# First attention layer: the queries' products run beside the key norm and the index heads' products, with banks dealt anew and another order on VectorE

## The chip, the cores and the metric

One NeuronCore of a Trainium2 chip runs the whole program. The metric is the device time of one execution in microseconds (us). The engines have queues of their own and meet at semaphores: TensorE (PE in the profile; PEld is its weight load), VectorE (DVE), ScalarE (ACT), GpSimd (POOL), and SyncE (SP), which issues the weight loads. TensorE writes to PSUM, of which there are eight banks of 512 fp32 columns; VectorE and ScalarE read them.

## What is computed

Two transformer blocks one after the other, each of depth 2, on 256 tokens of width 1024 in fp32. The change is in the first layer of the first block, sparse attention over 272 positions (16 meta tokens and 256 tokens; 384 with padding, which the kernel leaves out):

```python
q, k, v, qi, ki, wi = jnp.split(h @ w_in, list(A_SPLITS), axis=-1)
q = rope(rms_norm(q.reshape(B, T, A_Q_HEADS, HEAD_DIM), q_gain), cos, sin)     # 16 heads of 64
k = rope(rms_norm(k.reshape(B, T, A_KV_HEADS, HEAD_DIM), k_gain), cos, sin)    # 4 heads of 64
qi = rope(qi.reshape(B, T, IDX_HEADS, IDX_DIM), cos, sin)                      # 8 index heads of 64
ki = rope(ki[:, :, None, :], cos, sin)[:, :, 0, :]
...
logits = jnp.einsum('qhd,sd->qhs', qi_blk, ki_s)
score = jnp.einsum('qh,qhs->qs', w_blk, jax.nn.relu(logits))
score = jnp.where(causal, score, -jnp.inf)
_, idx = lax.top_k(score, topk)                                                # topk = 64
...
s = jnp.einsum('qgrd,qkgd->qgrk', q_blk, k_sel) * scale                        # softmax over the chosen keys, times v
```

After it come the output projection, the squared-relu MLP, a second layer with another attention, and the second block (short convolution, differential attention and two expert layers with gathered experts).

## The kernel before

*Layout.* Activations lie transposed, 128 features on the partitions and 272 positions along a row: `hTh` and `hTl` are the high and low parts of the normed input, eight chunks `kc` of 128 features each. Weights are streamed in groups `g` of four chunks `c` of 128 output columns (512 KB each) into a ring of two groups, `wring`. ScalarE makes a chunk's high part (`split_hi`, into `whi[:, c]`, which holds one group only), VectorE its low part (`split_lo`, into the place of the weights). A product is three matmuls (high times high, high times low, low times high) for each of eight `kc`: 24 matmuls, the function `chunk`, whose end raises `lin_done`. ScalarE's split of chunk c of group g waits until chunk c of group g-1 is done; SyncE's load of a chunk waits for the count of chunks done two groups earlier.

*The stage.* Groups 0 (`G_KI`), 1 (`G_QI`) and 2 (`G_KV`) give the index key, the index queries and key and value; groups 3 and 4 (`G_Q` and the next) the 16 query heads, in four pairs of chunks (a pair holds the first and second halves of four heads). Between groups 2 and 3 stand, in the queues of the engines:

- the key norm: ScalarE squares the key's two chunks (banks 0 and 1), PE sums them over heads (`pair_sums(0)`, line 753, bank 4), ScalarE takes the root (`pair_root(0)`, L1276, raises `pair_rt`), VectorE inverts it, scales the two chunks and rotates them (`pair_norm`, L1847 to L1653, raises `pair_done` to 1 and so frees banks 0 and 1);
- the index logits: 16 of them, eight heads for each of two blocks of 128 queries (n = 0 to 7 over 144 keys, n = 8 to 15 over 272). PE makes one with two fp32 matmuls on 32 rows (L773, L774; the rows' quarter is h % 4), in bank 4 + n % 4; ScalarE takes the relu (L1298) into one of two buffers `reluA`, when VectorE has used the one before last; VectorE adds it, weighted, to the score (L1878, raises `logit_used`);
- the queries, on PE: for n = 0 to 3 a chunk, the head sums of the pair before (`pair_sums(n)`, L758, twelve tiny matmuls as recorded), a chunk. The banks of the pairs are `Q_BANK` = 0, 2, 6, 0 and the next of each. ScalarE squares each chunk (L1269, L1271), takes the roots (L1279, L1280) and makes the high parts of group 4. VectorE makes the low parts of group 4 two at a time (L1616), rotates a pair (`rope_query`, L1859 to L1863) straight from the banks, and after the second pair does the selection for the first block of queries: eight rounds of the eight largest (L1701, L1702) and the mask (L1707, L1708);
- then `attention(0)`: scores (L580), masking on VectorE (L1726), the exponential (L1195), transposes (L611), values (L632). It waits for all pairs (`pair_done` 5). The selection for the second block lies inside it. Then the output projection (L664, fp32 matmuls).

PE waits for `pair_rt` 1 before the first logit and for all 16 relus before the first query chunk; `chunk` ends up behind both.

Of the kernel before, what the change touches and what calls it, by code (L numbers as in the profile page):

```python
# [127 lines left out]
def build(nc, xT_in, w_stream, wf_in, c_in, ada_w, tab_in, vec_in, alibi_in, subkeys, experts, lam_in, subln_in, out):  # L128
    ctx = ExitStack()
    with ctx:  # L130
# [302 lines left out]
        Q_BANK = (0, 2, 6, 0)  # L433
# [82 lines left out]
        def _(pe):  # L516
# [229 lines left out]
            def pair_sums(n):  # L746
# [7 lines left out]
                else:  # L754
                    heads = table("block32").rearrange("p (b c) -> p b c", b=4)[:, :, 0]
                    for r, (q0, nq) in enumerate(ROWS):
                        for half in range(2):
                            last = mm(banks[4 + n % 2][0:nq, 4 * r:4 * r + 4], sq_pair[:, n % 2, half, q0:q0 + nq], heads,  # L758
                                      start=half == 0, stop=half == 1)
# [4 lines left out]
            pe.wait_ge(pair_rt, 1)  # L764
            for n in range(2 * IDX_HEADS):
# [4 lines left out]
                if n >= 4:  # L770
                    pe.wait_ge(logit_relu, n - 3)
                bank = banks[4 + n % 4][:, 0:w]
# [3 lines left out]
            pe.wait_ge(logit_relu, 2 * IDX_HEADS)  # L776
            for n in range(4):
                g, c, b = G_Q + n // 2, 2 * (n % 2), Q_BANK[n]

                if n == 0:  # L780
                    pe.wait_ge(pair_done, 1)
                elif n == 1:
                    pe.wait_ge(v_ready, 3)
                elif n == 3:
                    pe.wait_ge(pair_done, 2)
                chunk(g, c, banks[b][:, 0:T], h_all)
                if n:
                    pair_sums(n)
                chunk(g, c + 1, banks[b + 1][:, 0:T], h_all)
# [316 lines left out]
        def _(act):  # L1106
# [158 lines left out]
            def pair_squares(n, g, c, b):  # L1265
                act.wait_ge(lin_done, CPT * g + c + 1)
                if n >= 2:
                    act.wait_ge(pair_ss, n - 1)
                link(af(sq_pair[:, n % 2, 0], banks[b][:, 0:T], ACT.Square))  # L1269
                act.wait_ge(lin_done, CPT * g + c + 2)  # L1270
                af(sq_pair[:, n % 2, 1], banks[b + 1][:, 0:T], ACT.Square).then_inc(pair_sq, 1)  # L1271

            def pair_root(n):
# [5 lines left out]
                af(q_root[0:N_META, 0, h], banks[4 + n % 2][0:N_META, 0:4], ACT.Sqrt, scale=1.0 / HD, bias=vcol("eps", 0)[0:N_META])  # L1279
                af(q_root[:, 1:3, h], banks[4 + n % 2][:, 4:12].rearrange("p (r b) -> p r b", r=2), ACT.Sqrt, scale=1.0 / HD,  # L1280
# [12 lines left out]
            for n in range(2 * IDX_HEADS):  # L1293
                w = sum(ROWS[1 + n // IDX_HEADS])
                act.wait_ge(logit_done, n + 1)
                if n >= 2:
                    act.wait_ge(logit_used, n - 1)
# [1107 lines left out]
```

## Time and profile before

| | us |
|---|---|
| median of 3 runs | 2399.63 (2394.72 to 2401.28) |
| profiled execution | 2395.71 |
| its span, first to last instruction | 2393.9 |
| stretch of the change, key sums to the first masked score | 61.92 to 115.06 |
| attention of this layer, to the output projection | 115.06 to 176.58 |

```profile
span 2393.9 us, 28234 instructions
...
PE   7779999998999998887777989987998997788776
...
DVE  5655677664778879767667476656657656676744
...
PEclk9889999989999998999999999999999999999999
```

The page cuts the span in 40 slices; each digit is the busy share of a slice in tenths, PEclk the granted TensorE clock. The stage of the change lies in the second slice (60 to 120 us). Times in the rows are us from the span's start. fp32 matmuls are recorded as two instructions each, matmuls of split values as one. Ends of matmuls are modelled, so step lengths are read from start to start.

### The profile page before, as it was taken

The page shows a single profiled execution, that of the slowest core. Times are in us where ns is not written, and L with a number is a line of the kernel's source. Part 1 is how long each engine was busy: PE and PEld are TensorE (multiplying, and loading weights), DVE is VectorE, ACT ScalarE, POOL GpSimd, SP SyncE. Part 2 cuts the span into 40 slices and gives each one's busy share as a digit, 9 for nine tenths or more (in the row PEclk, how much of TensorE's full clock was granted, in tenths as well). Part 3 has the DMA queues.
Part 4 walks back from the last instruction along what each step waited for, and adds up shares of the span by engine and source line. Part 5 has one row for each costly group of instructions (what it writes and reads, how often), then busy time and mean ns, then how long its engine had stood idle before and what let it go on. Part 6 is the DMA issues. An engine that isn't in the chain of part 4 may idle for free.

```text
span 2393.9 us, 28234 instructions
## 1 busy us (share of the span) xinstructions
PE 2093.9 (87%) x9740; PEld 1338.5 (56%) x9740; DVE 1591.5 (66%) x3698; ACT 1129.8 (47%) x2744; POOL 655.5 (27%) x624
## 2 busy tenths in 40 slices
PE   7779999998999998887777989987998997788776
PEld 7759999776999996443223434432444442233222
DVE  5655677664778879767667476656657656676744
ACT  4354534534653435444445375444457544444543
POOL 0000011110001005544443343343334344444441
PEclk9889999989999998999999999999999999999999
DMA  6205587751669756999999999999999999999995
GB/s 229 89 1 171 177 303 254 247 194 40 208 207 361 249 168 246 395 420 419 420 420 413 420 385 414 420 420 420 409 421 360 419 377 421 420 420 420 420 421 219
DMA packets 132100, 768.22 MB, mean 321 GB/s; under 512 B 14464, under 2 KB 17280, under 8 KB 60032
## 3 DMA queue, kind: packets, MB, share of 16 engines
q0 software_dynamic: 87552, 587.24, 60.3%
q1 hardware_dynamic: 43696, 177.81, 20.9%
q8 instruction: 71, 1.16, 0.2%
q10 hardware_dynamic: 720, 1.51, 0.2%
q14 instruction: 61, 0.50, 0.1%
HBM read 765.45 MB, written 1.05 MB: 320 GB/s over the span
## 4 chain that ended last, share of the span: by engine, by line
PE 52%; DMA 27%; DVE 10%; ACT 7%; issue 2%; POOL 1%; SPq 0%; ACTq 0%; POOLq 0%; DVEq 0%
DMA arena<-experts,arena 26%; PE bank L889 13%; PE bank L532 9%; PE bank L534 9%; PE bank L533 9%; PE bank L923 7%; DVE arena L2163 3%; PE bank L664 1%; ACT arena L1378 1%; ACT L1373 1%; ACT arena L1377 1%; ACT arena L1195 1%; POOL arena L498 1%; PE bank L632 1%; ACT L1449 1%
## 5 line engine op out<-in xcount | busy, mean ns | idle before, releaser
L889 PE MATMUL bank<-arena 128*128 128x512 f32 x2048 | 979.8, 616 | 165.0 <-ACT arena L1378 164.8
L2163 DVE CUSTOM_DVE_ANT_0 arena<-arena 128x1024 f32<-128x1024 f32 x512 | 633.4, 1239 | 465.4 <-DMA arena<-experts,arena 464.9
L498 POOL DMA_INDIRECT arena<-experts,arena x512 | 571.2, 1116 | 836.8 <-PE bank L889 794.9
L889 PEld LDWEIGHTS bank<-arena 128*128 128x128 f32 x2048 | 371.6, 193 | 725.4 <-ACT arena L1378 376.6
L1121 ACT CAST whi<-wring 128x1024 fp32r<-128x1024 f32 x228 | 238.2, 1049 | 271.8 <-PE bank L534 264.0
L1616 DVE TENSOR_TENSOR wlo<-wring,whi 128x1024 fp32r<-128x1024 f32 x216 | 263.3, 1224 | 144.9 <-ACT whi L1121 144.7
L1373 ACT ACTIVATE arena<-arena 128x1 f32<-128x1 f32 x512 | 102.9, 201 | 503.0 <-DVE arena L2163 501.4
L484 POOL DMA_DIRECT2D arena<-ada_w x64 | 34.2, 534 | 680.5 <-DVE adaM L1663 661.8
L1378 ACT ACTIVATE arena<-tab,arena 128x128 f32<-128x128 f32 x512 | 205.5, 401 | 16.7
L532 PE MATMUL bank<-hTh,whi 128*128 128x256 f32 (+1 forms) x576 | 172.2, 299 | 17.5 <-DVE hTl L1625 9.4
L533 PE MATMUL bank<-hTl,whi 128*128 128x256 f32 (+1 forms) x576 | 166.8, 290 | 0.0
L534 PE MATMUL bank<-hTh,wlo 128*128 128x256 f32 (+1 forms) x576 | 166.6, 289 | 0.0
L1377 ACT ACTIVATE arena<-arena 128x1 f32<-128x1 f32 x512 | 150.8, 295 | 16.7
L923 PE MATMUL bank<-wring,hfT 128*128 128x512 f32 x320 | 145.8, 599 | 3.3 <-DVE hfT L2100 3.3
L532 PE MATMUL bank<-mTh,whi 128*128 128x272 f32 (+1 forms) x512 | 146.2, 286 | 0.0
L533 PE MATMUL bank<-h1l,whi 128*128 128x272 f32 (+1 forms) x512 | 145.8, 285 | 0.0
L533 PE MATMUL bank<-mTl,whi 128*128 128x272 f32 (+1 forms) x512 | 145.8, 285 | 0.0
L532 PE MATMUL bank<-h1h,whi 128*128 128x272 f32 (+1 forms) x512 | 145.6, 284 | 0.0
L534 PE MATMUL bank<-h1h,wlo 128*128 128x272 f32 (+1 forms) x512 | 145.4, 284 | 0.0
L534 PE MATMUL bank<-mTh,wlo 128*128 128x272 f32 (+1 forms) x512 | 145.4, 284 | 0.0
L532 PEld LDWEIGHTS bank<-hTh,whi 128*128 128x128 f32 x576 | 112.6, 196 | 24.4 <-issue 18.2
L533 PEld LDWEIGHTS bank<-hTl,whi 128*128 128x128 f32 x576 | 112.9, 196 | 1.0 <-issue 1.0
(306 smaller groups left out, 3067.0 us busy)
## 6 DMA issues: line engine op xcount, KB each, us to landing
wring<-w_stream SPq DMA_DIRECT2D x236, 512.0 KB, 3.9
wring<-w_stream SPq DMA_DIRECT2D x48, 1024.0 KB
arena<-ada_w POOLq DMA_DIRECT2D x64, 512.0 KB, 5.3
alibi<-ada_w POOLq DMA_DIRECT2D x32, 512.0 KB, 5.5
arena<-experts,arena POOLq DMA_INDIRECT x512
xT<-xT_in SPq DMA_DIRECT2D x1, 1088.0 KB, 5.0
alibi<-alibi_in ACTq DMA_DIRECT2D x1, 1024.0 KB, 4.9
outT<-xT SPq DMA_DIRECT2D x2, 512.0 KB, 13.8
```

Of the source, the lines that this page charges most:

```text
L498: pool.indirect_dma_start(g_ring[:, r], None, experts[n // (2 * PEER_HEADS)], bass.IndirectOffsetOnAxis(idx[:, s // SLOTS % 2, s % SLOTS:s ...
L532: mm(dst, a[0], b[0], start=start, stop=False)
L533: mm(dst, a[0], b[1], start=False, stop=False)
L534: return mm(dst, a[1], b[0], start=False, stop=stop)
L889: last = mm(banks[2 * t + b][:, :], diag[:, r], g_ring[:, r, D + b * TILE_N:D + (b + 1) * TILE_N], start=s % SLOTS == 0, stop=s % SLOTS == ...
L923: last = mm(dst, lhs[:, 4 * half + k], w[:, k * TILE_N:(k + 1) * TILE_N], start=half == 0 and k == 0, stop=half == 1 and k == 3)
L1121: nc.scalar.copy(whi[:, c], wring[:, g % 2, c]).then_inc(hi_done, 1)
L1373: link(af(gel8[:, r:r + 1], act8[:, r:r + 1], ACT.Gelu))
L1377: link(af(coef8[:, r:r + 1], gel8[:, r:r + 1], ACT.Copy, scale=gate[:, s // SLOTS % 2, at:at + 1]))
L1378: af(diag[:, r], ident, ACT.Copy, scale=coef8[:, r:r + 1]).then_inc(diag_ready, 1)
L1616: v.tensor_tensor(wlo[:, g % 2, c], wring[:, g % 2, c], whi[:, c].bitcast(F32), ALU.subtract).then_inc(lo_done, 1)
L2163: v.tensor_tensor_reduce(g_ring[:, r, 0:D], g_ring[:, r, 0:D], hrow[:, t], 1.0, 0.0, ALU.mult, ALU.add, act8[:, r:r + 1]).then_inc(dot_don ...
```

## The change

- **PE.** The first two query chunks (group 3) follow `pair_sums(0)` at once, after a wait for the three value copies (`v_ready` 3), since they now go to banks 2 and 3. Then logits 0 and 1, the third chunk (bank 6), logits 2 and 3, `pair_sums(1)`, the fourth chunk (bank 7) with logits 4, 5 and 6 ahead of its `kc` 5, 6 and 7, and logit 7. Group 4: chunk 0 (bank 0, after `pair_done` 1) with logits 8 to 11 ahead of `kc` 4 to 7, `pair_sums(2)`, chunk 1 (bank 1) with logits 12 to 15 in the same way, then (after `pair_done` 2) chunks 2 and 3 in banks 2 and 3 with `pair_sums(3)` between, and `pair_sums(4)`.
- **Banks.** `Q_BANK` becomes 2, 6, 0, 2. Logits alternate between banks 4 and 5, so logit n waits for relu n - 2 rather than n - 4. The queries' head sums all go to bank 5, columns 288 on (`SUMS_AT`), behind the logits' 272.
- **ScalarE.** Squares, high parts of group 4, roots and relus are put in the order in which PE now makes them. The link between a pair's two squares is a wait before the second.
- **VectorE.** After the key norm: low parts 0 and 1 of group 4, the eight sums of the first block, rotation 1, low parts 2 and 3, the eight sums of the second block, rotation 2, the selection of the first block, rotations 3 and 4.

The number of instructions on each engine is the same. The diff, its core:

```diff
-        Q_BANK = (0, 2, 6, 0)
+        Q_BANK = (2, 6, 0, 2)
+        SUMS_AT = 288
...
-            pe.wait_ge(pair_rt, 1)
-            for n in range(2 * IDX_HEADS):
+            def logit(n):
...
-                if n >= 4:
-                    pe.wait_ge(logit_relu, n - 3)
-                bank = banks[4 + n % 4][:, 0:w]
+                if n == 0:
+                    pe.wait_ge(pair_rt, 1)
+                elif n >= 2:
+                    pe.wait_ge(logit_relu, n - 1)
+                bank = banks[4 + n % 2][:, 0:w]
...
-            pe.wait_ge(logit_relu, 2 * IDX_HEADS)
-            for n in range(4):
...
+            def beside(at):
+                return lambda kc: logit(at[kc]) if kc in at else None
+
+            pe.wait_ge(v_ready, 3)
+            chunk(G_Q, 0, banks[2][:, 0:T], h_all)
+            chunk(G_Q, 1, banks[3][:, 0:T], h_all)
+            logit(0)
+            logit(1)
+            chunk(G_Q, 2, banks[6][:, 0:T], h_all)
+            logit(2)
+            logit(3)
+            pair_sums(1)
+            chunk(G_Q, 3, banks[7][:, 0:T], h_all, beside({5: 4, 6: 5, 7: 6}))
+            logit(7)
+            pe.wait_ge(pair_done, 1)
+            chunk(G_Q + 1, 0, banks[0][:, 0:T], h_all, beside({4: 8, 5: 9, 6: 10, 7: 11}))
+            pair_sums(2)
+            chunk(G_Q + 1, 1, banks[1][:, 0:T], h_all, beside({4: 12, 5: 13, 6: 14, 7: 15}))
+            pe.wait_ge(pair_done, 2)
+            chunk(G_Q + 1, 2, banks[2][:, 0:T], h_all)
+            pair_sums(3)
+            chunk(G_Q + 1, 3, banks[3][:, 0:T], h_all)
             pair_sums(4)
...
+            pair_square(1, G_Q, 0, 0)
+            split_hi(G_Q + 1, 0)
+            pair_square(1, G_Q, 0, 1)
+            split_hi(G_Q + 1, 1)
+            logit_relus(0, 2)
+            pair_square(2, G_Q, 2, 0)
+            split_hi(G_Q + 1, 2)
+            pair_root(1)
+            logit_relus(2, 8)
+            pair_square(2, G_Q, 2, 1)
+            split_hi(G_Q + 1, 3)
+            logit_relus(8, 10)
+            pair_square(3, G_Q + 1, 0, 0)
+            pair_root(2)
+            logit_relus(10, 16)
+            pair_square(3, G_Q + 1, 0, 1)
+            pair_square(4, G_Q + 1, 2, 0)
+            pair_root(3)
+            pair_square(4, G_Q + 1, 2, 1)
             pair_root(4)
...
+            split_lo(G_Q + 1, 0)
+            split_lo(G_Q + 1, 1)
             dve.wait_ge(wi_ready, 1)
+            logits(1)
+            rope_query(1)
+            split_lo(G_Q + 1, 2)
+            split_lo(G_Q + 1, 3)
+            logits(2)
+            rope_query(2)
             dve.wait_ge(logit_used, 2 * IDX_HEADS)
-            for n in range(1, 5):
...
+            for _ in range(TOPK // 8):
+                select_round(1)
+            keys_selected(1)
+            rope_query(3)
+            rope_query(4)
```

## Rows read from the trace of the kernel before

**Rows 1.** the page's section 1: busy us, share of the span, instructions
```profile
PE 2093.9 (87%) x9740; PEld 1338.5 (56%) x9740; DVE 1591.5 (66%) x3698; ACT 1129.8 (47%) x2744; POOL 655.5 (27%) x624
```

**Rows 2.** busy us by stretch; columns: us, PE, PEld, DVE, ACT, POOL, PEclk, DMA
```profile
62.00:66.50 4.50, 1.00 (x5) 0.49 (x3) 2.37 (x3) 4.31 (x6) 0.00 (x0) 1.00 0.68 233
66.50:72.00 5.50, 2.04 (x24) 1.48 (x24) 5.36 (x10) 0.47 (x2) 0.00 (x0) 0.65 0.02 4
72.00:80.40 8.40, 7.42 (x41) 6.22 (x41) 6.09 (x15) 4.93 (x14) 0.00 (x0) 0.50 0.00 0
80.40:85.00 4.60, 4.60 (x20) 4.60 (x21) 0.55 (x2) 0.00 (x0) 0.00 (x0) 0.50 0.00 0
85.00:92.00 7.00, 7.00 (x59) 6.82 (x57) 1.64 (x2) 2.68 (x4) 0.00 (x0) 0.99 0.46 150
```

**Rows 3.** PE in order of time: start, us, line, xcount, idle before and its releaser
```profile
61.92 1.08 PE L753 MATMUL bank<-arena,tab 128*128 128x272 f32 x4
66.51 0.55 PE L773 MATMUL bank<-arena 32*128 32x144 f32 x8 [3.51 <-ACT rt L1276]
...
72.49 1.07 PE L773 MATMUL bank<-arena 32*128 32x144 f32 x3 [3.60 <-ACT arena L1298]
...
80.39 0.59 PE L532 MATMUL bank<-hTh,whi 128*128 128x272 f32 x1 [0.49 <-ACT arena L1298]
```

**Rows 4.** PE in order of time around pair_sums(1), full clock
```profile
91.57 0.29 PE L534 MATMUL bank<-hTh,wlo 128*128 128x272 f32 x1
91.78 1.24 PE L758 MATMUL bank<-tab,arena 128*16 128x4 f32 x12
92.89 0.37 PE L532 MATMUL bank<-hTh,whi 128*128 128x272 f32 x1
93.10 0.28 PE L533 MATMUL bank<-hTl,whi 128*128 128x272 f32 x1
...
93.48 0.29 PE L533 MATMUL bank<-hTl,whi 128*128 128x272 f32 x1
```

**Rows 5.** ScalarE in order of time, value copies and last square
```profile
62.12 0.65 ACT L1289 COPY arena<-bank 128x256 f32<-128x256 f32 x2 [2.48 <-PE bank L534]
...
110.91 0.40 ACT L1271 ACTIVATE arena<-bank 128x272 f32<-128x272 f32 x1 [2.50 <-PE bank L534]
```

**Rows 6.** VectorE in order of time, key norm to first masked score
```profile
71.21 0.43 DVE L1653 TENSOR_TENSOR arena<-arena 128x272 f32<-128x272 f32 x1
...
72.16 3.20 DVE L1878 SCALAR_TENSOR_TENSOR arena<-arena 128x144 f32<-128x144 f32 x7
...
76.68 1.71 DVE L1878 SCALAR_TENSOR_TENSOR arena<-arena 128x272 f32<-128x272 f32 x3
...
90.36 2.36 DVE L1616 TENSOR_TENSOR wlo<-wring,whi 128x1024 fp32r<-128x1024 f32 x2 [9.31 <-ACT whi L1121]
...
102.55 0.31 DVE L1701 MAX8 arena<-arena 128x8 f32<-128x144 f32 x1
...
109.17 1.73 DVE L1859 SCALAR_TENSOR_TENSOR arena<-bank,vec,tab 128x272 f32<-128x272 f32 x4
...
111.76 1.73 DVE L1859 SCALAR_TENSOR_TENSOR arena<-bank,vec,tab 128x272 f32<-128x272 f32 x4
...
115.06 0.16 DVE L1726 CUSTOM_DVE_ANT_0 arena<-bank,tab 16x16 f32<-16x16 f32 x1
```

**Rows 7.** chain of waits, fp32 matmuls of the output projection
```profile
176.58 29.60 PE bank L664 x128
```

**Rows 8.** PE, 272-column scores on 32 rows each, full clock
```profile
156.06 1.20 PE L580 MATMUL bank<-arena 32*128 32x272 f32 x16
```

**Rows 9.** shorter stretches, same columns; the last of PE alone
```profile
74.90:78.30 3.40, 3.40 (x25) 3.09 (x21) 2.28 (x5) 1.59 (x4) 0.00 (x0) 0.50 0.00 0
...
115.90:119.30 3.40, 0.83 (x20) 0.61 (x20) 3.05 (x23) 3.04 (x16) 0.00 (x0) 0.50 0.01 2
...
160.30:163.70 3.40, 1.54 (x14) 1.00 0.00 0
```

More of the change, by code:

```diff
@@ L756, in pair_sums @@
                     for r, (q0, nq) in enumerate(ROWS):
+                        at = SUMS_AT + 16 * (n - 1) + 4 * r
                         for half in range(2):
-                            last = mm(banks[4 + n % 2][0:nq, 4 * r:4 * r + 4], sq_pair[:, n % 2, half, q0:q0 + nq], heads,
+                            last = mm(banks[5][0:nq, at:at + 4], sq_pair[:, n % 2, half, q0:q0 + nq], heads,
                                       start=half == 0, stop=half == 1)
@@ L1263, in _, with pair_square @@
             act.wait_ge(v_zero, 1)
-            def pair_squares(n, g, c, b):
-                act.wait_ge(lin_done, CPT * g + c + 1)
-                if n >= 2:
+            def pair_square(n, g, c, half):
+                b = Q_BANK[n - 1] if n else 0
+                act.wait_ge(lin_done, CPT * g + c + half + 1)
+                if half == 0 and n >= 2:
                     act.wait_ge(pair_ss, n - 1)
-                link(af(sq_pair[:, n % 2, 0], banks[b][:, 0:T], ACT.Square))
-                act.wait_ge(lin_done, CPT * g + c + 2)
-                af(sq_pair[:, n % 2, 1], banks[b + 1][:, 0:T], ACT.Square).then_inc(pair_sq, 1)
+                if half:
+                    act.wait_ge(act_seq, seq[0])
+                    af(sq_pair[:, n % 2, 1], banks[b + 1][:, 0:T], ACT.Square).then_inc(pair_sq, 1)
+                else:
+                    seq[0] += 1
+                    af(sq_pair[:, n % 2, 0], banks[b][:, 0:T], ACT.Square).then_inc(act_seq, 1)
             def pair_root(n):
@@ L1292, in _, with logit_relus @@
             pair_root(0)
[L1293 to L1297, printed above, removed]
-                af(reluA[:, n % 2, 0:w], banks[4 + n % 4][:, 0:w], ACT.Relu).then_inc(logit_relu, 1)
-            for n in range(1, 5):
-                g, c = G_Q + (n - 1) // 2, 2 * ((n - 1) % 2)
-                if n >= 2:
-                    pair_root(n - 1)
-                pair_squares(n, g, c, Q_BANK[n - 1])
-                if g + 1 < G_AOUT:
-                    split_hi(g + 1, c)
-                    split_hi(g + 1, c + 1)
+            def logit_relus(n0, n1):
+                for n in range(n0, n1):
+                    w = sum(ROWS[1 + n // IDX_HEADS])
+                    act.wait_ge(logit_done, n + 1)
+                    if n >= 2:
+                        act.wait_ge(logit_used, n - 1)
+                    af(reluA[:, n % 2, 0:w], banks[4 + n % 2][:, 0:w], ACT.Relu).then_inc(logit_relu, 1)
+            pair_square(1, G_Q, 0, 0)
[17 more added lines that the diff above has]
+            pair_square(4, G_Q + 1, 2, 1)
             pair_root(4)
```

47 lines of the change are left out of this document (15 added, 32 removed).

## The prediction

> **What bounds the kernel now.** First the page: TensorE is busy 87% of the span, VectorE 66% [rows 1]. Such a share is a mean over stages and says little about one. The change touches one stage only, so I read that stage by stretches. The keys', values' and index work before it fills PE; then, from 62.0 to 80.4, PE does 1.00 us of work in 4.50, 2.04 in 5.50 and 7.42 in 8.40, and its granted clock goes from 1.00 (2.4 GHz) to 0.50 (1.2 GHz); 0.50 holds to 85.1; from there to 110.8 PE is full at 1.00 [rows 2]. PE's order of time names the two holes: 3.51 us on the root of the key norm (ScalarE) and 3.60 us on a relu that VectorE had not made room for, since VectorE was in the key norm until 71.6 [rows 3, 6]. The queries' eight chunks start only at 80.39. VectorE in turn idles 9.31 us at 81.1 to 90.4 for want of chunks, and from the selection at 102.55 on runs almost without a hole to the first masked score at 115.06 [rows 6]. So the stage ends like this: PE late, last square at 110.91, last query rotation on VectorE 111.76 to 114.35, scale of the queries to 115.06, attention.
>
> **Part by part.** All times are of the profiled execution (2395.71 us, span 2393.9; the median of the runs is 2399.63, 3.9 us more, by which I shift at the end).
>
> *Start of the queries.* The first chunk now needs the value copies, which end at 62.77, and PE is done with `pair_sums(0)` at 61.92 + 4 x 0.23 = 62.84 [rows 3, 5]. The low parts of group 3's chunks 0 and 1 are long made, those of 2 and 3 end at 66.1, before their turn. So the chunks start at 62.84 instead of 80.39, 17.5 us earlier, and the clock has no hole to fall in: the 21 matmuls that took 0.23 us each at 80.4 to 85.1 take 0.126 [rows 2, 4], 2.1 us less.
>
> *Logits inside the chunks.* What moves into PE's queue ahead of the later chunks are 16 logits, two fp32 matmuls each, which the trace records as four instructions. Before, neighbours with different heads ran on different quarters of the rows and overlapped: 16 such instructions of 272 columns took 1.20 us at full clock in the scores [rows 8], 0.30 us for the four of one logit. Now each is alone between full-array matmuls, or behind one neighbour. The nearest row for a lone one is the 272-column fp32 matmul at full clock, 128 records in 29.60 us, 0.231 each [rows 7]: 4 x 0.23 = 0.91 us per logit of the second block, and in proportion 0.49 us for 144 columns. Entering and leaving a group of small matmuls adds something: around `pair_sums(1)` the steps are 0.21 us where 0.126 is the rule, on either side, 0.17 us together [rows 4]. No row shows it for a logit. Bounds: 0.15 and 0.30 us (full overlap; I see no cause for less), and 0.66 and 1.08 us with the whole 0.17 (beyond that, a drain of the array each time: 0.75 and 1.20). I take +0.10, so 0.59 and 1.01 us.
>
> The Trainium skill, "TensorE: Matmul & The Clock Gate", Part 3 (Packing small matmuls), says that matmuls of 32 rows run together when they sit in different row groups, and that a single one takes as long as one of 128 rows. That speaks against this change, which takes them apart. The scores' 1.20 us agree with its first half, and no row here shows a lone one at full clock; by its second half the price is the 0.91 used above.
>
> *PE up to the last logit.* Five whole chunks 5 x 3.02 = 15.1 us, `pair_sums` 1 and 2 at 1.26 (start to start beyond the chunks' own step) = 2.5, seven eighths of the sixth chunk 2.65, logits 8 x 0.59 + 8 x 1.01 = 12.8: 33.1 us, so logit 15 leaves PE at about 95.9. I went through the waits on the way in that order: ScalarE's relu of logit n-2, which frees the bank of logit n, is always past (the nearest are logits 6 and 12, by some 0.7 us); `pair_done` 1 comes at 71.6, chunk 0 of group 4 starts at about 81; VectorE's low part of group 4's chunk 0 is made at 72.8; the first query rotation (`pair_done` 2) ends at about 84.6 and is wanted at 96.3.
>
> *ScalarE* gets no instruction more; it waits in another order. Behind its wait for chunk 4 stand root 2 and the relus from 10 on, and VectorE waits some 2 us there; that lies inside the time in which PE is late anyway. The table load before the key root is as before.
>
> *VectorE* works off, after the key norm: 4 low parts, 16 logit sums, rotations 1 and 2, selection, rotations 3 and 4. By the rows (7 sums of 144 columns in 3.20, 3 of 272 in 1.71, two low parts 2.3 start to start, a rotation 109.17 to 111.76) that is, without a wait, 2.3 + 8 x 0.46 + 2.59 + 2.3 + 8 x 0.60 + 2.59 + 6.62 + 2 x 2.59 = 30.0 us from 71.6: 101.6, and 0.7 for the scale of the queries. This is the floor, 102.3 against 115.06. But logit 15 comes late. Its relu is ready at 96.6 (0.27 from matmul to ScalarE, 0.4 for it), the sum ends at 97.2, and behind it VectorE has a tail with nothing left to hide it: rotation 2 (2.59), eight selection rounds and the mask (102.55 to 109.17: 6.62), rotations 3 and 4 (5.17), scale (0.7) [rows 6]. 97.2 + 15.1 = **112.3**. Before, the selection lay under PE's chunks at no cost; this is the cover that goes. PE's last chunk is done at about 103.9, its last sums at 105.6, and then it waits 6 us for VectorE.
>
> The same walk, with the half-clock steps, applied to the kernel before gives 114.9 for its 115.06, so I compare walk with walk: 114.9 - 112.3 = **2.5 us gained**. The 17.5 + 2.1 us of PE come back as 12.8 us of logits, and of the rest all but 2.5 is lost to VectorE's tail.
>
> *Weight loads and SyncE.* The loads wait for chunk counts, whose order is unchanged. They come earlier, and the next that PE could miss (group 7) waits for the output projection, after attention. Nothing. GpSimd has no work here. *Banks.* The query sums share bank 5 with odd logits; a price for writing a bank while it is read is in no row; I take 0, with up to 1 us on top.
>
> *Attention after it.* It has the same instructions (61.5 us to 176.58). Its clock is 0.50 from 115.9 to 139.8 [rows 2, 9]. With PE idle beforehand the fall comes a bit earlier, on tiny matmuls, and the return may move by a few us either way: -1 to +2 us. Value 0.
>
> Sum: 2395.7 - 2.5 = 2393.2 for an execution like the profiled one; on the median, **2397.1**.
>
> **Rivals.**
> *(a) The logits stay cheap* (0.15 and 0.30 us): something in PE still overlaps them with their neighbours. The walk then gives 103.2, 11.6 us gained, 2388.0. For it speaks only the scores' row; against it, that each stands between matmuls that use all rows.
> *(b) Switching is dearer or attention's clock returns later.* At 0.75 and 1.20 us the walk gives 115.1, no gain: PE's two holes come back spread over 16 logits. 2398 to 2401. For it: the 0.17 us steps.
> *(c) Slower: the clock falls in the mixed stretch.* Chunks 4 and 5 are about 70% logits by time. In 74.9 to 78.3 PE was busy all of 3.40 us with logits and the clock stayed at 0.50; it rose only after a dense chunk [rows 2, 9]. If it falls to 0.50 when chunk 4 starts and stays, 16 chunk steps cost 0.30 us more each and 8 logits 0.91: 4.9 + 7.3 = 12.2 us on the path that ends at logit 15, 124.5 against 114.9, 9.7 slower, 2409.3. The sign turns after 5 us at half clock (half of it is lost). Against it: with only 1.54 us of matmuls in 3.40 at 160.3 to 163.7 the clock stayed at 1.00 [rows 9], and the mixed stretch holds about 1 us of dense matmuls in that time plus the logits.
> The same page, Part 1, says that idle gaps of PE bring the lower clock back; by it the wait before attention would too, which the trace already shows for the gap at 110.8 [rows 2, 9] and which changes no price here.
> *(d) It doesn't do what it says:* PE still held up by the key norm. The diff has no wait on `pair_rt` ahead of the first two chunks, so I leave this out.
>
> **Numbers.** Forecast 0.60 (2393 to 2400 by itself, run spread included: 2394.72 to 2401.28); (b) 0.20; (a) 0.11; (c) 0.09, of which 0.06 past the bound. A measurement of this kernel can tell about 0.3%, 7.2 us, from no change. Faster by more than that: only (a) and a bit of the forecast's edge, 0.12. Slower: 0.06. Within: 0.82. Range for 8 in 10: from near (a) to past (b): 2389 to 2404.
>
> **What would show it.** PE without a hole from 61.9 to about 104, clock 1.00 throughout; lone second-block logits 0.9 to 1.1 us apart from chunk step to chunk step; the last logit relu at about 96.3; VectorE waiting on ScalarE's relus between 74 and 97, then with no hole to about 112.3; PE idle some 6 us before the first score, released by VectorE's rotation; attention 61.5 us long within 2. It is wrong if the last logit is much before 95 (a), if the clock reads 0.50 before 104 (c), or if VectorE's tail is not the last thing ahead of the first score.

## The result, and the profile after

The changed kernel took 2408.61 us (median of 20; 2402.76 to 2413.19) against 2397.72 of the kernel before (median of 20; 2392.89 to 2405.80): ratio 1.0040, 95% interval 1.0032 to 1.0048, so 0.4% slower, 9.6 us by the ratio. The profiled execution has a span of 2407.2 us. In it the key sums stand at 65.18, the first masked score at 122.92 and the output projection at 186.29: the stage took 57.7 us where before took 53.1, attention 63.4 where it took 61.5. I call "stage" here and below the time from the key sums (first record of the fp32 `pair_sums(0)`) to the first masked score, since what lies ahead of it moves from one execution to the next. One execution of all those recorded, one of the twelve of the kernel with earlier pairs below, took 2663.68 us at a mean granted clock of 0.741 and is left out of its figures.

The same view as [rows 2], the changed kernel by stretches (us, PE, PEld, DVE, ACT, POOL, PEclk, DMA share, GB/s):

```profile
62.00:66.50 4.50, 4.50 (x36) 4.17 (x35) 0.00 (x0) 1.49 (x4) 0.00 (x0) 1.00 0.05 9
...
85.00:92.00 7.00, 7.00 (x35) 4.97 (x34) 6.07 (x11) 1.98 (x4) 0.00 (x0) 1.00 0.19 73
92.00:100.00 8.00, 8.00 (x35) 6.57 (x34) 1.00 (x2) 1.40 (x6) 0.00 (x0) 0.57 0.18 66
100.00:107.00 7.00, 7.00 (x22) 4.20 (x22) 1.51 (x3) 1.18 (x4) 0.00 (x0) 0.68 0.00 0
107.00:113.00 6.00, 6.00 (x27) 5.95 (x27) 5.29 (x17) 0.77 (x2) 0.00 (x0) 0.51 0.27 90
113.00:120.00 7.00, 5.72 (x50) 5.26 (x48) 6.55 (x23) 1.93 (x7) 0.00 (x0) 0.98 0.39 136
```

Both holes of [rows 3] are gone: PE is full from 62 to 113. But the clock reads 0.57, 0.68 and 0.51 between 92 and 113, where the fifth to seventh chunk run, and PE has no hole there (8.00 us busy in 8.00, 7.00 in 7.00): it goes through 35 matmuls in 8 us at 92 and 22 in 7 us at 100. In the trace's record of the clock it is 0.50 from 92.3 to 99.2 and from 102.6 to 112.8. Before the first fall PE did logits 8 to 11, one ahead of each step of the chunk; before it came back at 99.2, head sums and four steps of the sixth chunk in a row (95.36 to 98.36).

PE in order of time, the start of the queries, with logits 0 and 1 side by side:

```profile
65.18 1.08 PE L754 MATMUL bank<-arena,tab 128*128 128x272 f32 x4
66.08 0.39 PE L533 MATMUL bank<-hTh,whi 128*128 128x272 f32 x1
...
72.10 0.29 PE L535 MATMUL bank<-hTh,wlo 128*128 128x272 f32 x1
72.32 0.52 PE L777 MATMUL bank<-arena 32*128 32x144 f32 x4
72.67 0.42 PE L778 MATMUL bank<-arena 32*128 32x144 f32 x4
73.02 0.39 PE L533 MATMUL bank<-hTh,whi 128*128 128x272 f32 x1
73.25 0.29 PE L534 MATMUL bank<-hTl,whi 128*128 128x272 f32 x1
```

The chunks start 0.90 us after the key sums, as forecast. Below, a matmul of a chunk takes 0.126 us from start to start at the full clock, and a step of the chunk (one `kc`) is three of them, 0.38 us. The two adjacent logits of 144 columns stretch the row of the chunk's matmuls (72.10 to 73.25, less two of 0.126) by 0.90 us, both together. Now a lone one of 272 columns, logit 8 ahead of the fifth step of chunk 4:

```profile
86.05 0.29 PE L535 MATMUL bank<-hTh,wlo 128*128 128x272 f32 x1
86.27 0.72 PE L777 MATMUL bank<-arena 32*128 32x272 f32 x2
86.84 0.62 PE L778 MATMUL bank<-arena 32*128 32x272 f32 x2
87.38 0.39 PE L533 MATMUL bank<-hTh,whi 128*128 128x272 f32 x1
87.61 0.29 PE L534 MATMUL bank<-hTl,whi 128*128 128x272 f32 x1
```

From 86.05 to 87.61 there are 1.56 us where two matmuls of 0.126 would be: 1.31 us for one logit. The chunk's last matmul ahead of it takes 0.22 to the logit's start, the logit's second pair of records comes 0.57 after the first and the chunk's next matmul 0.54 after that, where two fp32 records last 0.46, and the matmul after that follows at 0.23: 0.39 us in all on top of 4 x 0.23. Lone logits of 144 columns stand 1.26 us apart, start to start, with a chunk step of 0.38 between: 0.88 us. VectorE's tail, which answers to [rows 6]:

```profile
107.40 0.50 DVE L1914 SCALAR_TENSOR_TENSOR arena<-arena 128x272 f32<-128x272 f32 x1 [2.58 <-ACT arena L1322]
107.82 1.72 DVE L1895 SCALAR_TENSOR_TENSOR arena<-bank,vec,tab 128x272 f32<-128x272 f32 x4
...
117.03 1.72 DVE L1895 SCALAR_TENSOR_TENSOR arena<-bank,vec,tab 128x272 f32<-128x272 f32 x4
...
119.62 1.73 DVE L1895 SCALAR_TENSOR_TENSOR arena<-bank,vec,tab 128x272 f32<-128x272 f32 x4
...
122.92 0.16 DVE L1762 CUSTOM_DVE_ANT_0 arena<-bank,tab 16x16 f32<-16x16 f32 x1
```

The last sum is 107.40 to 107.90; rotation 2, selection to 116.9, rotations 3 and 4, the scale, and the first masked score: 15.5 us from start to start, 15.7 forecast. PE waits 3.0 us for it, not 6, since it is later itself (view of the waits, 60 to 124 us):

```profile
PE bank L581 <- DVE arena L1899: 3.0, 1, 3.0
```

### The profile page after: what moved, and what is told of

Same layout as the page of the kernel before. It is cut to its first block, busy times and chain, and to the rows that moved or that the text cites. A ratio compares the mean times of both kernels' runs of the same rounds, so it can differ in the third digit from the quotient of the medians.

```text
span 2407.2 us, 28235 instructions
## 1 busy us (share of the span) xinstructions
PE 2117.4 (88%) x9740; PEld 1352.1 (56%) x9740; DVE 1591.2 (66%) x3698; ACT 1128.9 (47%) x2744; POOL 640.2 (27%) x624
## 3 DMA queue, kind: packets, MB, share of 16 engines
q1 hardware_dynamic: 43696, 177.81, 20.6%
## 4 chain that ended last, share of the span: by engine, by line
PE 55%; DMA 25%; DVE 8%; ACT 8%; issue 2%; POOL 1%; SPq 0%; ACTq 0%; POOLq 0%; DVEq 0%
DMA arena<-experts,arena 25%; PE bank L905 13%; PE bank L533 9%; PE bank L535 9%; PE bank L534 9%; PE bank L939 7%; DVE arena L2205 3%; PE bank L665 1%; ACT arena L1414 1%; ACT L1409 1%; ACT arena L1413 1%; POOL arena L499 1%; ACT arena L1211 1%; PE bank L633 1%; ACT L1485 1%
## 5 line engine op out<-in xcount | busy, mean ns | idle before, releaser
L499 POOL DMA_INDIRECT arena<-experts,arena x512 | 556.3, 1086 | 853.5 <-PE bank L905 812.2
```

The costliest lines, as they stand in the source:

```text
L499: pool.indirect_dma_start(g_ring[:, r], None, experts[n // (2 * PEER_HEADS)], bass.IndirectOffsetOnAxis(idx[:, s // SLOTS % 2, s % SLOTS:s ...
```

## The experiments

*The theories.* P: a lone logit on a quarter of the rows costs more than taken (0.88 and 1.31 us), PE is late by that. C: the clock falls because of such logits, and this makes the loss. D: VectorE's order, with the selection in its tail, makes it.

The walk of the prediction (times added up along the queues of PE, ScalarE and VectorE, each wait met by what ends it) was repeated for each kernel with the prices measured in these traces and a clock of 1.00. It is an estimate, and the yardstick of the table; "low" is the time in us at a granted clock of 0.50 inside the stage, from the record of the clock. In the kernels with the new order 1.8 to 5.9 us of it lie in the wait before attention, behind PE's own work (1.2 in the block, none with the selection early).

| kernel | stage, walk | stage, measured | low in it | attention | ratio to before (95%) |
|---|---|---|---|---|---|
| before | 52.9 | 53.1 | 17.1 | 61.5 | 1 |
| before, second profile | 52.9 | 53.7 | 22.4 | 64.0 | |
| before, third profile | 52.9 | 53.2 | 17.1 | 61.5 | |
| changed | 53.4 | 57.7 | 20.3 | 63.4 | 1.0040 (1.0032 to 1.0048) |
| changed, again | 53.4 | 57.8 | 20.6 | 63.2 | 1.0044 (1.0028 to 1.0060) |
| pairs | 46.1 | 46.1 | 5.9 | 61.5 | 0.9988 (0.9977 to 0.9999) |
| pairs, again | 46.1 | 46.1 | 4.9 | 64.0 | 0.9984 (0.9969 to 0.9998) |
| pairs, earlier | 45.8 | 48.5 | 12.0 | 64.0 | 0.9981 (0.9967 to 0.9996) |
| full rows | 48.9 | 48.7 | 5.0 | 64.0 | 1.0001 (0.9991 to 1.0011) |
| full rows, padded | 55.9 | 55.8 | 4.0 | 62.3 | 1.0020 (1.0003 to 1.0038) |
| block | 44.7 | 51.2 | 14.8 | 62.1 | 1.0012 (0.9999 to 1.0025) |
| block on full rows | 47.9 | 48.0 | 4.0 | 62.3 | 0.9986 (0.9970 to 1.0002) |
| selection early | 51.3 | 62.3 | 30.7 | 61.6 | 1.0041 (1.0025 to 1.0057) |
| spread | 54.1 | 71.8 | 51.1 | 63.4 | 1.0039 (1.0016 to 1.0061) |

(Before's walk has its half-clock steps in it, so its 17.1 us don't stand against it.)

The table has one profile of each kernel or two. The mean granted clock is on record for every execution, and tells how long each ran at half clock. Averaged over the executions of a kernel that is 185 and 182 us for the changed kernel, 181 for the block, 183 with the selection early; 187 for the spread logits; 175, 176 and 174 for the kernel before beside them; 170 and 168 for the pairs, 174 for the earlier ones; 167, 166 and 172 for the three kernels with logits on all rows. Each is known to 2 to 6 us. So the difference between lone logits on a quarter of the rows and logits on all rows is in the executions without a profile too.

### Logits in pairs

```diff
-            chunk(G_Q, 3, banks[7][:, 0:T], h_all, beside({5: 4, 6: 5, 7: 6}))
-            logit(7)
+            chunk(G_Q, 3, banks[7][:, 0:T], h_all, beside({5: (4, 5), 7: (6, 7)}))
...
-            chunk(G_Q + 1, 0, banks[0][:, 0:T], h_all, beside({4: 8, 5: 9, 6: 10, 7: 11}))
+            chunk(G_Q + 1, 0, banks[0][:, 0:T], h_all, beside({4: (8, 9), 6: (10, 11)}))
...
-            chunk(G_Q + 1, 1, banks[1][:, 0:T], h_all, beside({4: 12, 5: 13, 6: 14, 7: 15}))
+            chunk(G_Q + 1, 1, banks[1][:, 0:T], h_all, beside({4: (12, 13), 6: (14, 15)}))
```

> The changed kernel, but the logits from the fourth on stand in pairs instead of alone: 4 and 5, 6 and 7 in the fourth chunk, 8 and 9, 10 and 11 in the fifth, 12 and 13, 14 and 15 in the sixth. Neighbours of a pair are on different quarters of the rows. Theory P (price of a lone logit): in the changed kernel's trace a lone logit lengthens the chunk by 1.31 us (272 columns) or 0.88 us (144), while the two adjacent ones at 72.3 us cost 0.90 us together. So a pair should cost about 0.90 or 1.33 us, as much as one alone: six visits less, the walk through the queues ends the stage 7.3 us earlier than in the changed kernel, total 7 to 10 us below the changed kernel. Theory D (VectorE's order, with the selection in its tail, is the cause): VectorE's tail is untouched, total within 2 us of the changed kernel. Theory C (the clock alone): the price per pair is of no matter, the clock still falls to 0.50 in the fifth and sixth chunk, total 0 to 4 us below the changed kernel.

PE in order of time around logits 8 and 9, and VectorE's first masked score, of this kernel:

```profile
80.50 0.29 PE L535 MATMUL bank<-hTh,wlo 128*128 128x272 f32 x1
80.72 0.73 PE L777 MATMUL bank<-arena 32*128 32x272 f32 x4
81.28 0.63 PE L778 MATMUL bank<-arena 32*128 32x272 f32 x4
81.84 0.39 PE L533 MATMUL bank<-hTh,whi 128*128 128x272 f32 x1
...
107.49 0.16 DVE L1761 CUSTOM_DVE_ANT_0 arena<-bank,tab 16x16 f32<-16x16 f32 x1
```

From 80.50 to the last matmul before the next pair, at 82.58, there are 2.08 us, less six matmuls of 0.126: 1.32 us for two logits, as much as one alone cost. The stage is 46.1 us, on the walk, the clock 1.00 until PE's end at 100.9 (it falls at 101.6). Total 2392.50 us against 2396.21, and 12.5 us below the changed kernel by the two ratios of 1.0040 and 0.9988. That is more than P foresaw (7 to 10) and much more than D did (within 2), so D falls: VectorE's order is the same here. The clock, which by C should have fallen all the same, held. So price and clock changed together, and this run alone doesn't part them: of the 11.6 us by which the stage is shorter than the changed kernel's, 7.3 are price by the walk and 4.3 the clock.

### Logits on all 128 rows

```diff
-                mm(bank, qiA[g, 2 * (h // 4), q0:w], kiA[g, 0, 0:w], start=True, stop=False)
-                mm(bank, qiA[g, 2 * (h // 4) + 1, q0:w], kiA[g, 1, 0:w], start=False, stop=True).then_inc(logit_done, 1)
+                mm(bank, qiA[:, 2 * (h // 4), q0:w], kiA[:, 0, 0:w], start=True, stop=False)
+                mm(bank, qiA[:, 2 * (h // 4) + 1, q0:w], kiA[:, 1, 0:w], start=False, stop=True).then_inc(logit_done, 1)
```

> The changed kernel, but each logit's two matmuls take all 128 rows instead of 32, so that they sum four heads: the scores are not the reference's (that part of the computation is changed), the columns, the order and all waits are the same. Theory C (the clock falls because matmuls on a quarter of the rows do not hold it): the granted clock reads 1.00 through the mixed stretch, no chunk step of 0.23 us in it, total 3 to 6 us below the changed kernel. Theory P with the switch between quarter rows and full rows as its cause: the price of a logit falls from 1.31 to about 0.91 + 0.17 = 1.08 us, another 3 us. If the price is that of fp32 between split values whatever the rows, it stays at 1.31. If the clock falls all the same, the rows are not what it looks at.

PE in order of time around one logit, then PE by stretches (us, PE, PEclk, DMA share, GB/s), of this kernel:

```profile
82.58 0.29 PE L535 MATMUL bank<-hTh,wlo 128*128 128x272 f32 x1
82.71 0.62 PE L777 MATMUL bank<-arena 128*128 128x272 f32 x2
83.17 0.62 PE L778 MATMUL bank<-arena 128*128 128x272 f32 x2
...
83.88 0.29 PE L535 MATMUL bank<-hTh,wlo 128*128 128x272 f32 x1
...
84.00:88.00 4.00, 4.00 (x30) 1.00 0.08 14
88.00:92.00 4.00, 4.00 (x27) 1.00 0.32 117
92.00:96.00 4.00, 4.00 (x27) 1.00 0.10 16
```

82.58 to 83.88 is 1.30 us, less three matmuls of 0.126 is 0.92 us: exactly four fp32 records, no switch at all, where P had put 1.08. So the 0.4 us belong to going between quarter rows and full rows, not to fp32 beside split values. The clock is 1.00 through the same mixture, and PE has no hole in either kernel up to its last 0.49 us wait, at 102.0 here and at 117.5 in the changed kernel. The stage is 48.7 us, total 2396.06 against 2396.21. This kernel comes near the one that the prediction described (it took 0.59 and 1.01 us a logit; here it is 0.49 and 0.92, at a clock of 1.00). Even so the total is level with before's (1.0001), though the stage is 4.4 us shorter.

### All logits in one block

```diff
-            logit(0)
-            logit(1)
             chunk(G_Q, 2, banks[6][:, 0:T], h_all)
-            logit(2)
-            logit(3)
             pair_sums(1)
-            chunk(G_Q, 3, banks[7][:, 0:T], h_all, beside({5: 4, 6: 5, 7: 6}))
-            logit(7)
...
+            chunk(G_Q, 3, banks[7][:, 0:T], h_all)
+            pe.wait_ge(pair_rt, 2)
+            for n in range(2 * IDX_HEADS):
+                logit(n)
             pe.wait_ge(pair_done, 1)
-            chunk(G_Q + 1, 0, banks[0][:, 0:T], h_all, beside({4: 8, 5: 9, 6: 10, 7: 11}))
+            chunk(G_Q + 1, 0, banks[0][:, 0:T], h_all)
+            pe.wait_ge(logit_relu, 2 * IDX_HEADS)
             pair_sums(2)
...
             logits(1)
+            logits(2)
             rope_query(1)
             split_lo(G_Q + 1, 2)
             split_lo(G_Q + 1, 3)
-            logits(2)
             rope_query(2)
```

(ScalarE's order follows; the logits of the sixth chunk are taken out in the same way.)

> One part of the change alone: the first four query chunks run ahead of the logits, with the new banks, but the 16 logits then stand in one block (two banks), followed by the other four chunks; VectorE sums all logits before the first rotation. No logit is inside a chunk. Theory P: the logits overlap again and cost about 9 us in all, the walk ends the stage 8.7 us before the changed kernel's and 8 us before the kernel before; total 2386 to 2395 where before is 2398. Theory D (the order on VectorE with the selection after PE's last sums): the selection is in the tail here too, so no gain over the kernel before. Theory C: the clock falls only if PE waits in the block; total some us above the first figure if it does.

The kernel by stretches, columns as above:

```profile
79.50:83.30 3.80, 2.79 (x24) 2.18 (x24) 2.21 (x6) 1.84 (x8) 0.00 (x0) 0.99 0.44 138
83.30:86.60 3.30, 2.82 (x11) 2.02 (x11) 1.17 (x3) 1.05 (x4) 0.00 (x0) 0.50 0.02 5
```

The walk's 44.7 us became 51.2. PE had only 2.79 us of work, all logits, in 79.5 to 83.3, and the clock then read 0.50 until 96.9: PE went on with logits, with holes of 0.2 to 0.3 us between every four matmuls, to 93.9. Total 2400.93 against 2396.21, ratio 1.0012. Of the gain that P foresaw 6.5 us are missing in the stage, and with all rows the same block stays on its walk (below): the clock took them.

### The selection early

```diff
             split_lo(G_Q + 1, 2)
             split_lo(G_Q + 1, 3)
+            dve.wait_ge(logit_used, IDX_HEADS)
+            for _ in range(TOPK // 8):
+                select_round(1)
+            keys_selected(1)
             logits(2)
             rope_query(2)
-            dve.wait_ge(logit_used, 2 * IDX_HEADS)
-            for _ in range(TOPK // 8):
-                select_round(1)
-            keys_selected(1)
             rope_query(3)
```

> The changed kernel, but VectorE makes the selection of the first block of queries (it needs logits 0 to 7 only) before the sums of the second block, in time in which it waits for relus. Theory P: the last logit is late whatever VectorE does; what is saved is only the part of the tail that lies behind PE's own end, 2 us by the walk: total 1 to 3 us below the changed kernel. Theory D: the whole selection of 6.6 us leaves the path, total 6 us or more below the changed kernel.

```profile
92.00:96.00 4.00, 4.00 (x15) 2.54 (x15) 3.59 (x14) 0.40 (x1) 0.00 (x0) 0.50 0.00 0
...
112.00:116.00 4.00, 4.00 (x19) 4.00 (x19) 3.73 (x9) 0.56 (x2) 0.00 (x0) 0.50 0.40 131
```

(By stretches, as above.) The ratio is that of the changed kernel, 1.0041: neither D's 6 us nor P's 1 to 3 are there. But the run says little of either, since the clock moved too: in this profiled execution the stage was 62.3 us, 11 over its walk, with the clock at 0.50 from 82.8 to 116.9 but for 3.4 us. What rules D out is the run with pairs.

### The changed kernel again

> The changed kernel itself once more, beside the others on one chip, for a second look at its clock. Theory C+P (a lone quarter-row logit costs 1.31 and 0.88 us, and the clock falls in the mixed stretch on top): the stage from the key sums to the first masked score is 53.4 us by the walk plus what the low clock adds, 57.7 in the first look; the fall lies again between the fifth and the seventh chunk, though not at the same instruction. Total 9 to 12 us above the kernel before.

2409.53 us against 2400.00 on the same chip, 1.0044. Stage 57.8 us; the clock was 0.50 from 91.2 to 98.0 and from 101.4 to 111.7, at the same two places as in the first profile (92.3 to 99.2, 102.6 to 112.8).

### The block on full rows

The edits of the block and of the full rows together.

> The kernel with all 16 logits in one block, but each logit on all 128 rows, so that no two overlap (scores not the reference's, that part of the computation is changed). Theory C: the clock reads 1.00 in the block and after it, where the quarter rows had 0.50 from 83.3 to 96.9; the stage is 47.9 us by the walk against 51.2 measured with quarter rows, though PE's own work in the block is longer; total 3 us or more below the block with quarter rows. If the clock follows PE's idle time alone, the result is the other way round: the block gets 2 to 4 us longer, since the overlap is gone.

```profile
80.00:84.00 4.00, 3.37 (x25) 2.94 (x24) 2.15 (x6) 2.23 (x7) 0.00 (x0) 1.00 0.40 131
84.00:88.00 4.00, 4.00 (x20) 3.31 (x20) 1.96 (x6) 1.77 (x5) 0.00 (x0) 1.00 0.02 4
```

(By stretches, as above.) The clock is 1.00 in and after the block. The stage is 48.0 us, 3.2 less than with quarter rows though the logits no longer overlap, and the total 2395.90 against 2400.00. The two blocks differ in nothing but the rows in the program. In the trace the holes differ too: with quarter rows 2.79 us of work in 3.80, here 3.37 in 4.00. So this pair alone leaves room for PE's idle time. The changed kernel and the one on full rows don't: PE has no hole in either before the clock falls in one of them, and in the other it doesn't fall.

### Pairs, earlier in their chunks

```diff
-            chunk(G_Q, 3, banks[7][:, 0:T], h_all, beside({5: (4, 5), 7: (6, 7)}))
+            chunk(G_Q, 3, banks[7][:, 0:T], h_all, beside({3: (4, 5), 6: (6, 7)}))
...
-            chunk(G_Q + 1, 0, banks[0][:, 0:T], h_all, beside({4: (8, 9), 6: (10, 11)}))
+            chunk(G_Q + 1, 0, banks[0][:, 0:T], h_all, beside({2: (8, 9), 5: (10, 11)}))
...
-            chunk(G_Q + 1, 1, banks[1][:, 0:T], h_all, beside({4: (12, 13), 6: (14, 15)}))
+            chunk(G_Q + 1, 1, banks[1][:, 0:T], h_all, beside({1: (12, 13), 4: (14, 15)}))
```

> The kernel with logits in pairs, each pair placed two or three steps of the chunk earlier (4 and 5 ahead of step 3, 6 and 7 ahead of 6, then 2 and 5, then 1 and 4). By the walk the stage is 45.8 us where the pairs had 46.1: no difference to be measured, total about 2392, unless the clock falls on the denser mixture, which would cost 3 us or more.

```profile
92.00:96.00 4.00, 4.00 (x17) 0.50 0.00 0
96.00:100.00 4.00, 4.00 (x18) 0.50 0.00 0
```

(PE by stretches.) The clock did fall, 90.7 to 101.0, and the stage took 48.5 us for a walk of 45.8. Total 2395.52 us against 2400.00, ratio 0.9981: no difference from the pairs that the intervals show. So pairs don't hold the clock wherever they stand.

### The lone logits spread

```diff
-            chunk(G_Q, 3, banks[7][:, 0:T], h_all, beside({5: 4, 6: 5, 7: 6}))
-            logit(7)
+            chunk(G_Q, 3, banks[7][:, 0:T], h_all, beside({1: 4, 3: 5, 5: 6, 7: 7}))
...
-            chunk(G_Q + 1, 0, banks[0][:, 0:T], h_all, beside({4: 8, 5: 9, 6: 10, 7: 11}))
+            chunk(G_Q + 1, 0, banks[0][:, 0:T], h_all, beside({1: 8, 3: 9, 5: 10, 7: 11}))
...
-            chunk(G_Q + 1, 1, banks[1][:, 0:T], h_all, beside({4: 12, 5: 13, 6: 14, 7: 15}))
+            chunk(G_Q + 1, 1, banks[1][:, 0:T], h_all, beside({1: 12, 3: 13, 5: 14, 7: 15}))
```

> The changed kernel, with the same lone logits on quarter rows, but spread: one ahead of steps 1, 3, 5 and 7 of the fourth, fifth and sixth chunk, instead of one ahead of each of the last steps. The number of lone visits and their price stay as in the changed kernel, and the last logit stands at the same step 7; the walk gives the stage 54.1 us, 0.7 more than for the changed kernel. Theory P alone: total as the changed kernel or 1 us above. Theory C+P: with dense steps between the logits the clock holds or falls later, stage 54 to 56 us instead of 57.7 and more, total 4 to 8 us below the changed kernel, near the kernel before.

```profile
76.00:80.00 4.00, 3.82 (x32) 3.00 (x30) 2.76 (x6) 2.07 (x6) 0.00 (x0) 0.90 0.39 134
80.00:84.00 4.00, 4.00 (x16) 3.47 (x16) 0.74 (x2) 0.58 (x2) 0.00 (x0) 0.50 0.00 0
...
120.00:124.00 4.00, 4.00 (x16) 3.30 (x15) 2.40 (x6) 0.80 (x2) 0.00 (x0) 0.50 0.17 39
```

(By stretches, as above.) A miss: 4 to 8 us below the changed kernel were expected, and the ratio is as the changed kernel's. The clock fell at 79.2, when the first of the spread logits had only begun: ahead of it stood logits 2 and 3, the head sums, one step of the chunk and a hole of 0.18 us. It came back only at 127.0, behind the first stretch of chunk steps without a logit (from 121.03). Before that there were never more than two steps in a row, where the changed kernel's clock had come back behind four. That the spacing kept it low is argued from this. The stage took 71.8 us in this execution, 18 over the walk. But it is the slowest of nine, which go from 2396.3 to 2423.4 us, a spread of 27 us where before's was 13 to 20. The slowest has a mean granted clock of 0.954, the fastest 0.965, which makes 223 and 168 us at half clock. An estimate from these: 55 us more at half speed cost up to 27 us, the whole spread. The executions between follow this loosely (0.966 at 2406.16). The median is 2407.75, ratio 1.0039.

### Full rows with the price of quarter rows

```diff
                 mm(bank, qiA[:, 2 * (h // 4), q0:w], kiA[:, 0, 0:w], start=True, stop=False)
+                for _ in range(2):
+                    mm(banks[4 + n % 2][:, 0:112], qiA[:, 2 * (h // 4), q0:w], kiA[:, 0, 0:112], start=False, stop=False)
```

> The price of a lone quarter-row logit without its rows: every logit takes all 128 rows (as in the run on full rows, where it cost 0.92 and 0.49 us), and two matmuls of 112 columns each are added to it, four recorded instructions of about 0.1 us, so that it costs about 1.31 and 0.88 us like the lone ones of the changed kernel. The scores are not the reference's (that part is changed, and work is added). If price and clock add up (C+P): the clock reads 1.00 up to PE's end, the stage is 53.4 us by the walk, as long as before's 53.1, total within 3 us of the kernel before; the 9 to 11 us of the changed kernel are then the clock's. If the price alone made the loss (P): total 8 us or more above the kernel before, as the changed kernel.

The diff is against the kernel on full rows. PE in order of time around a logit of 144 columns, then PE by stretches:

```profile
81.91 0.29 PE L535 MATMUL bank<-hTh,wlo 128*128 128x272 f32 x1
82.03 0.41 PE L777 MATMUL bank<-arena 128*128 128x144 f32 x2
82.28 0.59 PE L779 MATMUL bank<-arena 128*128 128x112 f32 x4
82.71 0.42 PE L780 MATMUL bank<-arena 128*128 128x144 f32 x2
...
83.22 0.29 PE L535 MATMUL bank<-hTh,wlo 128*128 128x272 f32 x1
```

```profile
104.00:108.00 4.00, 4.00 (x32) 1.00 0.35 123
```

A logit costs 0.93 us here (81.91 to 83.22 less three matmuls) and 1.36 with 272 columns, and the adjacent ones don't overlap, 0.96 us more for each of two couples. With these prices the walk gives 55.9 us, and 55.8 were measured, clock 1.00 to PE's end. Taking the excess out again (2 x 0.96, and 0.05 for 12 lone ones) leaves 53.3: at full clock the changed kernel's stage would be as long as before's, by this estimate. The total, 2405.98 against 2398.93, ratio 1.0020, is 4.8 us by the ratio, more than the 3 us I had allowed, with 2.7 us of stage to explain it. Its interval (0.7 to 9.1 us) holds 3 as well as 8, so the total doesn't decide between the two theories; the stage, on its walk at the full clock, does. What is not covered is taken up below.

### The pairs again

> The kernel with logits in pairs from the fourth on, a second time. C+P: stage 46.1 us where the clock holds, some 7 us shorter than before's; total 3 to 8 us below the kernel before, ratio 0.997 to 0.999. If the first result was luck of the clock, the ratio is 1.000 or above.

2395.41 us against 2398.93, ratio 0.9984 (0.9969 to 0.9998), stage 46.1 us again, mean clock 0.9649 against 0.9637 for before's executions beside it. The first result was not luck.

### The kernel before, two more profiles

> The kernel before once more, for its profile: all kernels with the new order took 2 to 4 us more in total than their stage alone accounts for against the one profile of before. If that one profile was lucky ahead of the stage and in attention, a second look shows the key sums at 63 to 65 us rather than 61.9 and attention of 62 to 64 us rather than 61.5. If the surplus belongs to the new order, the second look repeats 61.9 and 61.5. The stage itself should be 53 us again.

> The kernel before a third time, for the same question: key sums at 63 to 65 us and attention of 62 to 64 us if the first profile was lucky, 61.9 and 61.5 if not; stage 53 us with the clock at 0.50 for some 17 us in it.

PE's key sums and, from the chain of waits, the output projection in the second profile:

```profile
65.00 1.08 PE L753 MATMUL bank<-arena,tab 128*128 128x272 f32 x4
...
182.73 29.60 PE bank L664 x128
```

The two executions took 2405.47 and 2398.48 us. Key sums at 65.00 and 63.97, stage 53.7 and 53.2, attention 64.0 and 61.5. So the first profile was at the lucky end, ahead of the stage by 2 to 3 us: it had 6.8 us at half clock there, these two have 17.1 and 13.7. Comparisons of spans between two profiles carry that much chance; before's stage moved by 0.6 us at most. Attention is 61.5 us with 23.9 us at half clock in it, 62.3 with 26.7, 63.3 with 30.8 and 64.0 with 32.2 to 32.7, whatever the kernel.

## Why the prediction was wrong, point by point

- **Bottleneck and start of the queries: right.** The two holes of [rows 3] are gone; the chunks start 0.90 us after the key sums.
- **Price of a logit: the term of the sum that was mis-sized.** 0.59 and 1.01 us taken, 0.88 and 1.31 measured, beyond every bound I gave (0.75 and 1.20). This is the first half of rival (b), which I gave 0.20, at more than its own prices. The base of 0.49 and 0.91 was exact, as the full rows show (0.49 and 0.92); the switch was taken from [rows 4], where small matmuls stand on all rows (0.17 us), and I put it at 0.10. A switch between quarter rows and full rows and back costs 0.39 us here and stands in none of the rows ahead of the prediction. With the measured price the walk gives 53.4 us for the stage instead of 50.4: the 2.5 us of gain become a loss of 0.5. It also shows that two adjacent logits cost as much as one; the overlap that [rows 8] shows was there to be had.
- The Trainium skill, "TensorE: Matmul & The Clock Gate", section "Why this matters for your kernels", says that a matmul of 32 rows alone takes as long as one of 128. Where it stands alone between matmuls on all rows, the measurement differs: 1.31 us for the logit on 32 rows, 0.92 on 128. Part 3 of the same page of the Trainium skill (Packing small matmuls) says that matmuls in different row groups run together; the trace agrees, by the pair's 1.32 us.
- **Clock 1.00 up to PE's end: wrong, and this is the larger part.** The clock fell where rival (c) put it, in the mixed stretch of chunks 4 and 5 (the fifth and sixth in order). That (c)'s 2409.3 meets the measured 2408.61 is luck: by the walk the clock cost 4.3 us in the stage (57.7 against 53.4), not 12.2, since it was back at 1.00 from 99.2 to 102.6 and from 112.8; the dearer logits added 3.0 and some 3 us lie outside stage and attention. I gave (c) 0.09 on the strength of 1.54 us in 3.40 at 160.3 to 163.7 with the clock at 1.00 [rows 9]. Those were transposes on all 128 rows; I counted busy time and not rows. The row for it lay beside it: 3.40 us of logits in 3.40, clock 0.50. The changed kernel and the one on full rows have the same order and the same waits, and PE has no hole in either up to 102.0 and 117.5; the clock reads 0.50 for 17 us before PE's end in one and never in the other.
- **VectorE's tail: right.** 15.5 us from the last sum to the first masked score, 15.7 forecast. That it was the last thing ahead of attention is also right, but PE waits 3.0 us for it, not 6.
- **ScalarE, weight loads, banks: right,** as far as the walk with measured prices meets the stage in the five profiles with the clock at 1.00 to PE's end (pairs twice, full rows, padded, block on full rows) within 0.2 us. None of them shows a price for writing a bank while it is read, which I had put at 0.
- **Attention:** 63.4 us is inside the -1 to +2 allowed; the three profiles of before give 61.5 to 64.0, so it isn't shown that the change moved it.

**What stays open.** Stage and attention account for 4.6 + 1.9 = 6.5 us of the 9.6 by the ratio. In the pairs a stage 7 us shorter gave 2.9 and 3.8 us in total, on full rows 4.4 gave none, in the padded kernel 2.7 cost 4.8, and the block, with a stage 2.0 shorter, cost 2.9. So most kernels with the new order take 2 to 6 us more than their stage explains, and no profile locates these (the earlier pairs and the early selection lack less than 1; of the spread logits the slowest execution was profiled). Outside the stage the profiled executions take from 2337.9 to 2353.1 us, before's three from 2340.8 to 2350.0: one profile for each can't settle it.

The mean clocks point at the clock outside the stage. Less the low time in the profiled stage, the half-clock times above leave 157 to 159 us for before and 161 to 168 for the kernels that lack something: 2 to 12 us more, which at half speed cost 1 to 6 (an estimate). But each figure is uncertain by 2 to 4 us, and the earlier pairs have 162 too and lack nothing. That is argued, not shown.

Open too is what it is in the logits on quarter rows that the clock goes with: the rows themselves, or the 0.39 us that each lone one spends on the switch. The kernels on full rows change both. For the rows speaks that in the kernel before, at 74.9 to 78.3, logits ran among their like without a hole, and the clock, low already, stayed at 0.50 [rows 9].

## What to carry to other kernels

Work put into a hole is paid for where it stands: count what it costs there, alone between other instructions, not what it cost among its like. Small matmuls on part of TensorE's rows belong side by side in couples on different rows, with dense work around them: here the same logits, in pairs instead of alone, turned 0.4% slower into 0.1 to 0.2% faster than the kernel before. And a busy PE isn't a full clock: look whether its work is on all rows, and read the granted clock of every stretch that is mostly something else. A shorter stage isn't a shorter kernel either: 7 us less in it gave 3 to 4 in total.

## What the runs showed of the hardware that I had not expected

- Going from matmuls on all rows to one logit (four records on the same quarter of the rows) and back costs 0.39 us: 0.22 and 0.23 us for matmuls of 0.126, and 0.11 and 0.08 us more than their two records behind each of the logit's two matmuls. On full rows the same logit costs 0.92 us, with no such loss.
- The same columns in the same order, on a quarter of the rows or on all of them: in the changed kernel the clock was 0.50 from 92.3 to 99.2 and from 102.6 to 112.8, on full rows 1.00 to PE's end; in the block 0.50 from 83.3 to 96.9, on full rows 1.00 through it. The block on full rows is 3.2 us faster in the stage though PE has more to do.
- All rows alone don't hold the clock. In the kernel before 48 matmuls on all rows, of 8 columns each, ran from 28.5 to 33.9 us without a hole in PE (7.00 us busy from 27 to 34), and the clock was 0.50 from 34.0 to 37.4.
- One program, the one with spread logits, differed by 27 us between nine executions (2396.3 to 2423.4). In the slowest the clock was 0.50 for 47.8 us on end, 79.2 to 127.0.
